# The first block's borders by token tiles: token-major projection first, w_out, join, norm and turn of one tile beside the other's products

## What is computed

```python
def first_block(x, ...):
    for l in range(DEPTH):                                  # DEPTH = 2
        h = _rms_norm(x, norm_mix_pre[l])
        proj = jnp.einsum('bsd,de->bse', h, w_in[l])        # q, k, v of two attentions, low ranks, gates
        ...
        mixed = jnp.einsum('bsd,de->bse', jnp.sum(gates * br, axis=2), w_out[l])
        x = x + _rms_norm(mixed, norm_mix_post[l])

        h = _rms_norm(x, norm_mlp_pre[l])
        u = jnp.square(jax.nn.relu(jnp.einsum('bsd,df->bsf', h, w_up[l])))
        x = x + _rms_norm(jnp.einsum('bsf,fd->bsd', u, w_down[l]), norm_mlp_post[l])
    return x
```

## Time and profile before

| | us |
|---|---|
| median of 3 runs | 1937.15 (1937.04 to 1937.23) |
| the profiled execution, its own time | 1935.02 |
| its span, first to last instruction | 1933.7 |
| TensorE busy in it | 1639.0 |

### The profile page before, as it was taken

One profiled execution on the slowest core, in us unless ns is written; L12 is line 12 of the kernel. 1 busy time (PEld: TensorE's weight loads), 2 busy tenths in 40 slices (PEclk: granted clock), 3 DMA queues, 4 the chain that ended last, 5 costly groups with the idle time before them and its releaser, 6 DMA issues.

```text
span 1933.7 us, 24178 instructions
## 1 busy us (share of the span) xinstructions
PE 1639.0 (85%) x10180; PEld 1448.2 (75%) x10180; DVE 1166.8 (60%) x1958; ACT 754.6 (39%) x1187; POOL 50.1 (3%) x50
## 2 busy tenths in 40 slices
PE   7978997999798889879999876856499687999767
PEld 6868886999697788768998776755489666785445
DVE  5457556555645765455556765555887656867555
ACT  4445434444434443344444431312122143635224
POOL 0000010000000001100000001010000000000000
PEclk9979998999999999889998797966697688999879
DMA  8433334555544333345556320000002135341023
GB/s 266 151 109 109 110 109 153 175 183 187 177 153 148 109 112 110 101 143 192 182 188 199 109 88 28 17 0 0 1 1 88 39 109 194 122 129 44 1 97 115
DMA packets 150890, 219.87 MB, mean 114 GB/s; under 512 B 6197, under 2 KB 110653, under 8 KB 150141
## 3 DMA queue, kind: packets, MB, share of 16 engines
q1 hardware_dynamic: 150780, 218.33, 35.0%
HBM read 217.25 MB, written 1.06 MB: 113 GB/s over the span
## 4 chain that ended last, share of the span: by engine, by line
PE 71%; DVE 17%; ACT 6%; DMA 3%; issue 1%; POOL 0%; SPq 0%; DVEq 0%; ACTq 0%
PE bank L380 17%; PE bank L382 16%; PE bank L381 16%; PE bank L1733 4%; DVE weights_low L356 3%; PE bank L821 2%; PE bank L1824 2%; PE bank L2949 2%; PE bank L1992 2%; ACT weights_high L343 1%; PE bank L1790 1%; DVE place L2176 1%; PE bank L2975 1%; PE bank L458 1%; PE bank L1970 1%
## 5 line engine op out<-in xcount | busy, mean ns | idle before, releaser
L356 DVE TENSOR_TENSOR weights_low<-place,weights_high 128x1024 fp32r<-128x1024 f32 (+2 forms) x387 | 446.6, 1196 | 223.7 <-ACT weights_high L343 223.2
L343 ACT ACTIVATE weights_high<-place 128x1024 fp32r<-128x1024 f32 (+2 forms) x387 | 378.2, 1029 | 151.0 <-DMA place<-w_down_dram 42.9
L380 PE MATMUL bank<-hT_high,weights_high 128*128 128x256 f32 x1152 | 337.5, 293 | 6.0 <-DVE hT_low L477 4.4
L382 PE MATMUL bank<-hT_high,weights_low 128*128 128x256 f32 x1152 | 330.0, 286 | 0.0
L381 PE MATMUL bank<-hT_low,weights_high 128*128 128x256 f32 x1152 | 329.7, 286 | 0.0
L380 PEld LDWEIGHTS bank<-hT_high,weights_high 128*128 128x128 f32 x1152 | 222.9, 193 | 12.7 <-DVE hT_low L477 5.5
L381 PEld LDWEIGHTS bank<-hT_low,weights_high 128*128 128x128 f32 x1152 | 222.7, 193 | 0.8
L382 PEld LDWEIGHTS bank<-hT_high,weights_low 128*128 128x128 f32 x1152 | 222.2, 193 | 0.0
L1733 PE MATMUL bank<-place,place 128*128 128x128 f32 x624 | 91.3, 313 | 63.2 <-DVE place L2122 26.8
L1733 PEld LDWEIGHTS bank<-place,place 128*128 128x128 f32 x624 | 87.6, 225 | 67.9 <-issue 53.3
L382 PE MATMUL bank<-weights_high,branchT_low 128*128 128x512 f32 x256 | 101.0, 395 | 0.0
(11 more groups left out here) (412 smaller groups left out, 3385.4 us busy)
## 6 DMA issues: line engine op xcount, KB each, us to landing
place<-w_in_dram SPq DMA_DIRECT2D x48, 1024.0 KB, 5.3
place<-w_up_dram SPq DMA_DIRECT2D x32, 1024.0 KB, 5.4
place<-w_down_dram SPq DMA_DIRECT2D x32, 1024.0 KB, 5.0
place<-even_w_in_dram SPq DMA_DIRECT2D x17, 1024.0 KB, 5.2
place<-w_out_dram SPq DMA_DIRECT2D x16, 1024.0 KB, 5.2
place<-odd_w_in_dram SPq DMA_DIRECT2D x16, 1024.0 KB, 5.4
place<-w_branch_dram SPq DMA_DIRECT2D x12, 1024.0 KB, 5.0
place<-ple_gate_dram SPq DMA_DIRECT2D x8, 1024.0 KB, 5.1
```

The lines of the kernel that those rows point to most:

```text
L343: nc.scalar.activation(high[:, lo:hi], self.raw[p % SLOTS][:, lo:hi], ACT.Copy).then_inc(*A("high", p, j))
L356: nc.vector.tensor_tensor(low[:, lo:hi], self.raw[p % SLOTS][:, lo:hi], high[:, lo:hi].bitcast(FP32), ALU.subtract).then_inc(*V())
L380: nc.tensor.matmul(out, left[0], right[0], start=first, stop=False)
L382: return nc.tensor.matmul(out, left[1], right[0], start=False, stop=last)
```

## The change

The border's steps are made for each token tile apart. In the first layer's and second layer's list of projections the value projection n = 2 (token-major) comes first, `PROJECTIONS = (2, 0, 1, 3, 4, 5)`. `first_projection_tensor` turns tile 0, makes the first half of tile 0's products, turns tile 1, and then the rest. `w_out_by_tiles_tensor` makes both column halves of tile 0, then those of tile 1; the turn of tile 0 stands ahead of the last quarter of tile 1's products. Join and norm run by tile on ScalarE and VectorE, all sums of squares on ScalarE. The four calls that cut weights around w_out stand together ahead of the join, where before two stood ahead of each half. The rows of norm_mlp_pre and norm_mlp_post have places of their own and are loaded ahead of w_out's last two pieces, that of norm_mix_pre of the next layer too.

```diff
+PROJECTIONS = (2, 0, 1, 3, 4, 5)
...
-        k.load_beyond(("wo", l, 1, 1))
-        SP.wait_ge(("weighed", "mix", l, 1, 1), ("headsT", l, 2, 3))
-        nc.sync.dma_start(f.pre, row("norm_mlp_pre", l)).then_inc(*rows())
-        nc.sync.dma_start(f.post, row("norm_mlp_post", l)).then_inc(*rows("mlp_rows_loaded", l))
-        k.load_beyond(("down", l, TURNS - 1, 1))
+        k.load_up_to(("wo", l, 0, 1))
+        SP.wait_ge(("headsT", l, 2, 3))
+        nc.sync.dma_start(f.mlp_pre, row("norm_mlp_pre", l)).then_inc(*rows())
+        nc.sync.dma_start(f.mlp_post, row("norm_mlp_post", l)).then_inc(*rows("mlp_rows_loaded", l))
+        if l + 1 < DEPTH:
+            nc.sync.dma_start(f.pre, row("norm_mix_pre", l + 1)).then_inc(*k.pre_loaded("pre_loaded", l + 1))
+        k.load_beyond(("down", l, 0, 1))
+        SP.wait_ge(("weighed", "mix", l, 1, 1))
...
+def w_out_by_tiles_tensor(k, f, l):
+    T = k.T
+    for t in range(TT):
         for half in range(2):
-            k.token_major(("wo", l, half), k.halves_of(("wo", l, half)), f.hT, WB, lambda t, kk: [("mixed", l, kk // 2 * 2)])
-        k.turn_tensor(("normed", "mlp", l), split(f.flat_junk, TT, D), KT, [[("normed_by", "mlp", l, t)] for t in range(TT)])
-        mlp_tensor(k, f, l)
+            b = k.claim("wo", l, half, t)
+            for j, (name, m) in enumerate(k.halves_of(("wo", l, half))):
+                if (t, half, j) == (1, 1, 1):
+                    turn_normed_tensor(k, f, ("mlp", l), 0)
+                p, w = k.weights(name, m, WB)
+                for kk in range(j * m, (j + 1) * m):
+                    T.wait_ge(("mixed", l, kk // 2 * 2))
+                    ins = k.product(b, [part[:, kk, t * P:(t + 1) * P] for part in f.hT], [part[:, kk - j * m, :] for part in w],
+                                    kk == 0, kk == KT - 1)
+                if j:
+                    ins.then_inc(*T("wo", l, half, t))
+                elif t == 1:
+                    ins.then_inc(*T())
+                if t == 1:
+                    T.same("used", p)
+def first_projection_tensor(k, f, l):
+    T, n = k.T, PROJECTIONS[0]
+    h_ready = k.turned("normed", "mix", l)
+    turn_normed_tensor(k, f, ("mix", l), 0)
+    for t in range(TT):
+        b = k.claim("v", l, n, t)
+        for j, (name, m) in enumerate(k.halves_of(("v", l, n))):
+            if (t, j) == (0, 1):
+                turn_normed_tensor(k, f, ("mix", l), 1)
...
-    for n in range(6):
+    first_projection_tensor(k, f, l)
+    if l == 0:
+        rel_tensor(k, f)
...
@@ first_vector @@
-        for half in range(2):
+        for _ in range(4):
             k.low_of_next()
-            k.low_of_next()
-            weigh_vector(k, f, ("mix", l), half, [("wo", l, half, t) for t in range(TT)], ("post_loaded", l))
-        add_normed_vector(k, f, ("mix", l))
-        normed_vector(k, f, ("mlp", l), ("mlp_rows_loaded", l))
+        for t in range(TT):
+            for half in range(2):
+                weigh_vector(k, f, ("mix", l), f.post, half, t, ("wo", l, half, t), ("post_loaded", l))
+            add_normed_vector(k, f, ("mix", l), t)
+            normed_vector(k, f, ("mlp", l), f.mlp_pre, t, ("mlp_rows_loaded", l))
...
@@ mlp_vector, after the last turn @@
+    weigh = lambda t: [weigh_vector(k, f, ("mlp", l), f.mlp_post, half, t, ("mlp", l, t, half), ("mlp_rows_loaded", l)) for half in range(2)]
+    weigh(0)
+    add_normed_vector(k, f, ("mlp", l), 0)
+    weigh(1)
+    if l + 1 < DEPTH:
+        normed_vector(k, f, ("mix", l + 1), f.pre, 0, ("pre_loaded", l + 1))
+    add_normed_vector(k, f, ("mlp", l), 1)
     V.same("layer_done", l)
+    if l + 1 < DEPTH:
+        normed_vector(k, f, ("mix", l + 1), f.pre, 1, ("pre_loaded", l + 1))
...
@@ first_scalar @@
-        for half in range(2):
+        for _ in range(4):
             k.high_of_next()
-            k.high_of_next()
-            weigh_scalar(k, f, ("mix", l), half, [("wo", l, half, t) for t in range(TT)])
-        k.rstd_scalar(("add", "mix", l), f.stats[:, 6:8])
-        normed_scalar(k, f, ("mlp", l), ("added_to_x", "mix", l, 0), ("added_to_x", "mix", l, 1))
+        for t in range(TT):
+            for half in range(2):
+                weigh_scalar(k, f, ("mix", l), half, t, ("wo", l, half, t))
+            k.rstd_scalar(("add", "mix", l, t), f.stats[:, 6 + t:7 + t])
+            normed_scalar(k, f, ("mlp", l), t, ("added_to_x", "mix", l, t))
```

More of the change, by code:

```diff
@@ new lines, in first_projection_tensor @@
+def first_projection_tensor(k, f, l):
[7 more added lines that the diff above has]
+                turn_normed_tensor(k, f, ("mix", l), 1)
+            p, w = k.weights(name, m, WB)
+            for kk in range(j * m, (j + 1) * m):
+                T.wait_ge(*h_ready(t, kk))
+                ins = k.product(b, [part[:, kk, t * P:(t + 1) * P] for part in f.hT], [part[:, kk - j * m, :] for part in w],
+                                kk == 0, kk == KT - 1)
+            if j:
+                ins.then_inc(*T("v", l, n, t))
+            elif t == 1:
+                ins.then_inc(*T())
+            if t == 1:
+                T.same("used", p)
@@ L939, in normed_vector @@
+        mlp_vector(k, f, l)
+def normed_vector(k, f, tag, weight, t, weight_loaded, pieces=0):
+    nc, V, stats = k.nc, k.V, f.stats
+    k.rstd_vector(("norm", *tag, t), stats[:, 50 + t:51 + t], stats[:, 48 + t:49 + t], D, EPS_RMS, ("square", *tag, t))
     V.wait_ge(V, weight_loaded)
-    for t in range(TT):
-        nc.vector.scalar_tensor_tensor(normed[:, t, :], x[:, t, :], f.stats[:, 2 + t:3 + t], f.pre, ALU.mult, ALU.mult
-                                       ).then_inc(*V("normed_by", *tag, t))
+    nc.vector.scalar_tensor_tensor(split(f.flat_junk, TT, D)[:, t, :], f.x[:, t, :], stats[:, 50 + t:51 + t], weight, ALU.mult, ALU.mult
+                                   ).then_inc(*V("normed_by", *tag, t))
@@ L943, in normed_vector, with weigh_vector @@
     for _ in range(pieces):
         k.low_of_next()
[L945 to L948 removed]
+    k.turn_vector(("normed", *tag), f.hT, KT, t)
+def weigh_vector(k, f, tag, post, half, t, use, post_loaded):
     nc, V = k.nc, k.V
[L950 to L955 removed]
@@ L1388, in mlp_scalar @@
             k.high_of_next()
-    for half in range(2):
-        weigh_scalar(k, f, ("mlp", l), half, [("mlp", l, t, half) for t in range(TT)])
-    k.rstd_scalar(("add", "mlp", l), f.stats[:, 6:8])
+    weigh = lambda t, half: weigh_scalar(k, f, ("mlp", l), half, t, ("mlp", l, t, half))
+    weigh(0, 0)
+    weigh(0, 1)
+    k.rstd_scalar(("add", "mlp", l, 0), f.stats[:, 6:7])
+    weigh(1, 0)
+    weigh(1, 1)
+    if l + 1 < DEPTH:
+        normed_scalar(k, f, ("mix", l + 1), 0, ("added_to_x", "mlp", l, 0))
+    k.rstd_scalar(("add", "mlp", l, 1), f.stats[:, 7:8])
+    if l + 1 < DEPTH:
+        normed_scalar(k, f, ("mix", l + 1), 1, ("added_to_x", "mlp", l, 1))
 def first_gpsimd(k, f):
```

104 lines of the change are left out of this document (44 added, 60 removed).

## The result

The changed kernel takes 1960.84 us (median of 4 runs, 1959.04 to 1964.3), the kernel before took 1937.1 beside it (4 runs, 1935.33 to 1937.23): ratio 1.0127, 95% interval 1.0109 to 1.0144, slower. The medians lie 23.7 apart.

A forecast was written before the change was run, and what follows sets the result against it. TensorE's own work is 71% of the span, so a border is worth only TensorE's waits. Terms 15.8 + 0.9 + 12.6 + 0.9 - 5.3 - 0.9 + 6.4 = +30.4 on 1935.0, plus 2.1 for the median: 1967.5 us, range 1957 to 1977.

The forecast's parts named there:

- `w_out`, first layer, +15.8: At the first layer's w_out border, the first mlp product starts at 349.9 instead of 334.08, 15.8 us later.
- L + 10.1: At w_out, tile 0's norm ends 10.1 us after L, the landing of the second w_up piece.
- Second layer, +12.6: At the second layer's w_out border, the first mlp product comes at 861.3 instead of 848.71, 12.6 us later.
- The clock behind the second wait, +0.9 each: Behind each w_out border, about 8 more matmuls run at 0.213 instead of 0.118, costing 0.9 us per layer.
- Mlp to the second layer, -5.3: At the second layer's entry, value products run while tile 1 is joined, saving 5.3 us, between 2.8 and 6.
- Mlp to the second block, -0.9: At the second block's entry, the first product starts near 1039.0 instead of 1039.88, saving 0.9 us, between 0 and 3.
- The start, +6.4: In the start, rel and the weight pieces behind it come later, costing 6.4 us, between 3 and 8.
- both of the forecast's waits: In the start, TensorE waits 2.7 and 2.8 us for the fifth and sixth low parts, near 43 and 48.
- The first rival: At w_out, the cuts don't hold the join: sum -1.6, 1935.5 us, or 1929 without the start's stall; chance 0.09.
- The second rival: In the start, the clock falls too: 3.8 us lost for each of two waits, +7.6, 1975 us; chance 0.09.
- The landing: At w_out, a w_up piece lands 5.4 us after issue; the skill's 6.15 would add 0.75 per layer, 1969.0.

The follow-up runs named there:

- e1: The changed kernel with only two of the four weight cuts ahead of the join, one more behind each tile's norm and turn; 1933.14 us, ratio 0.9984.
- e3: The kernel before, with all four weight cuts ahead of w_out's first squares; 1936.38 us, ratio to before 0.9998.
- e4: The changed kernel with w_out's products in the old order and both turns behind them, four cuts still together; 1941.72 us, ratio to before 1.0027.
- e9: The kernel before with only the row loads of the norms' weights moved as in the changed kernel; 1927.13 us, ratio to before 0.9957.
- e5: The changed kernel with its start wholly as in the kernel before; 1957.10 us, ratio to before 1.0102.
- e6: The changed kernel with the relative positions' product, the sines and the vector setup moved earlier in its start; 1957.69 us, ratio to before 1.0110.
- e8: The changed kernel with start and w_out border from the kernel before, keeping the MLP's two borders and early row loads; 1922.29 us, ratio to before 0.9926.
- e7: The changed kernel with the old start; at w_out only the second column half by tile, both turns last, cuts spread; 1924.63 us, ratio to before 0.9936.

## Why the prediction was right

The forecast was +30.4 on the profiled execution and 1967.5; measured are +26.1 and 1960.8. The sign, the places and the mechanism are those of the text; the differences are sizes.

- **`w_out`, first layer, +15.8: measured +14.9.** The chain held link by link. Shifted by the 5.3 that the start adds, the last product ahead of tile 0's turn was due at 326.2 and came at 326.4; the second landing was due at 328.8, and its cut begins at 329.54, 0.7 late; from there the sum gave L + 10.1 = 339.6, and the transposes start at 339.38; the second wait was to be 6.8 and is 6.63. What was off is the stretch between: the last 12 products were put at the half clock throughout, 5.1, and took 4.2 from 341.00, since the clock was back for the last six (0.23 apart). e1, e3 and e4 show the cause, not only the chain: each undoes one half of the pair.
- **Second layer, +12.6: measured +11.7**, for the same reason. The cuts did not bind earlier than the landing there either.
- **The clock behind the second wait, +0.9 each: +1.2 and -0.6.** Behind the mlp's first product 27 start 0.21 apart in the first layer where 16 did before, and 13 in the second where 20 did. The reason in the text (fewer transposes in the recovery) fits the first layer and not the second; this was the one term that came out with the other sign, and with the start it is the one most off.
- **Mlp to the second layer, -5.3: -5.8.** The size is right and a part of its reason was not told. Tile 0's norm was put at 521.2 without the 2.31 for the row that lay in the old chain; the text said of the moved row loads that they "cost nothing" and gave them no gain. e9 shows that they are worth more than all of the order by tile: at this border 4.4 come with them alone, and over the kernel 9.6. That is the step that failed, though the sum didn't suffer by it, and it was in the rows of the trace.
- **Mlp to the second block, -0.9: -0.6.** The last product of the mlp ends at 1058.90, and the clock held in part (8 transposes in 1.09 and 8 in 1.34, where 16 took 3.67). Yet the first product waits 1.73 for a low part where it waited 0.59: VectorE cuts both tiles together, at 1064.18, behind tile 1's join and two fills of 0.49.
- **The start, +6.4: +5.0.** SyncE issued the sixth piece at 40.81 where it had been 35.31, 5.5 later where 6.7 was forecast; rel stood at 29.52 and not 31.0. The eight transposes of tile 1's turn took 1.04, where the text took 1.84 from a border at half clock. One wait of 3.4, for the fifth piece's low part, took the place of two. Up to this place all idle time of TensorE is 3.8 more than before (23.3 against 19.5), and 1.7 more is lost at the lower clock; the rest is 0.6 less. e5 and e6 confirm the cause. That the 5.0 is so near owes something to chance: e1, with the same start, has both of the forecast's waits (3.02 and 2.39, for the fifth and the sixth piece) and stands 7.2 behind the kernel before, e4 6.4.

The first rival, that the cuts don't hold the join, priced that kernel at 1935.5, and it is what e1 built: 1933.1. Its border figures, +0.7 in the first layer and -2.5 in the second, compare with +2.9 and -2.75. The second rival, a fallen clock in the start, came in small. The windows of TensorE behind the 3.4 wait read

```profile
45.00:49.00 4.00, 3.75 (x22) 0.69 1.07 364
49.00:53.00 4.00, 4.00 (x32) 0.88 1.10 347
53.00:57.00 4.00, 4.00 (x36) 1.00 0.89 276
```

which is 4 x 0.31 and 4 x 0.12 below full, 1.7 us of lost time, where the rival had 3.8 for each of two waits.

The landing was the term between two prices. The second piece was issued at 323.69 and its cut begins at 329.54, 5.85 later; the transfers between 318 and 332 have a median of 5.7 from issue to landing, where the page of the profile has 5.4 over all `w_up` pieces, before and after. The Trainium skill, DMA: Bandwidth & Descriptors, section Bandwidth, has 6.15 for 1 MB issued from GpSimd, not from SyncE as here; an estimate by it puts the landing at 329.84. Neither figure was exact: the row's was 0.45 short for a piece with another one in flight, the page's 0.3 long.

## What to carry to other kernels

A wait on an in-order engine is paid by everything behind it: before reordering products, ask which buffer each piece needs and which product frees it, and place the work that reads a fresh piece behind the work that frees its slot. The early cuts alone cost nothing and the new order alone a few us, but their pair 27, so try such edits in pairs. And look for the small transfer that a norm waits for at its very end: three rows of 4 KB per partition, loaded too late, cost 9.6 us (5.0 of it plain waiting), where the order by tile gave 2.6 in the traces at the two borders where it gained.

## What the runs showed that was not expected

- **The clock's return behind a border follows no wait length seen here.** After 8.28 us idle and 16 transposes, e8's next products ran at 2.4 GHz from the first in both layers; after the same 8.29, e9's second layer ran at 1.2 (0.41 each); after 4.64, e7 had 22 products at 1.2; after 1.35, its transposes took 1.09, full rate. The Trainium skill, TensorE: Matmul & The Clock Gate, section What's actually happening, has activity release the clock; the runs agree that it falls in idle time and returns under work, but when it returns differed by up to 27 products, or 2.6 us, between kernels with the same work there (the first mlp: none at the lower clock in e8, 27 in the changed kernel). What decides it stays open.
- **The same start differed by up to 2.3 us between kernels.** e7 and e8 have one start; e7 stood at 108.99 and e8 at 107.75, all of it from the first 48 products. Over all eight kernels with the old start it is 2.3, over the three with the changed one 2.2. Differences of 2 us in 1930 between kernels are of this size, and e7 against e8 isn't settled by them.
- **The granted clock can read 1.00 where products run at half rate**: e5 and e7 between 17 and 22. Ahead of the first change in the record, count the products.
